# Convolution products moved from GpSimd to ScalarE, with the rotary sines, the even layer's decays, an odd layer's transposes, the layer norm's sums and the first loads rearranged

## The reference, cut to what matters

```
u = x * (1 + sc1) + sh1
proj = u @ w_in                                   # q, k, v, glu_in (1024), two gates (1024 each)
q, k = partial_rope(q, cos, sin), partial_rope(k, cos, sin)
attn = moba_attention(q, k, v)                    # 8 heads of 64, causal over 256 keys
h = a * sigmoid(g)                                # glu, 512 channels
h = depthwise_conv(h, dw_w, 31 taps, causal) + dw_b
y_conv = silu(layer_norm(h)) @ w_conv_pw
y = (sigmoid(g_attn) * (attn @ w_attn_br) + sigmoid(g_conv) * y_conv) @ w_out
x = layer_norm(ALPHA * x + (1 + gt1) * y)         # called ln{l}a below
u = x * (1 + sc2) + sh2
x = layer_norm(ALPHA * x + (1 + gt2) * (relu(u @ w_up)**2 @ w_down))   # ln{l}b
```

## Time and profile before

| | us |
|---|---|
| median of 3 runs | 1769.52 |
| lowest and highest | 1769.32, 1771.22 |
| the profiled execution's own time | 1772.76 |
| its span (first to last instruction) | 1770.9 |
| PE busy | 1732.9 |
| DVE busy | 1378.2 |
| ACT busy | 917.0 |
| POOL busy | 289.3 |

### The profile page before, as it was taken

The page is one execution under the profiler, slowest core; times in us unless marked ns, Lnnn a source line. Parts: engine busy times, 40 slices in busy tenths (PEclk is TensorE's granted clock), DMA queues, the critical chain, the costliest instruction groups (busy, mean ns, idle before and its releaser), DMA issues.

```text
span 1770.9 us, 26710 instructions
## 1 busy us (share of the span) xinstructions
PE 1732.9 (98%) x11234; PEld 1555.7 (88%) x11234; DVE 1378.2 (78%) x1851; ACT 917.0 (52%) x1137; POOL 289.3 (16%) x219
## 2 busy tenths in 40 slices
PE   8999999999999999999999999999999999999998
PEld 7888998888888888879888898898888998998887
DVE  7998754798788988787988779888755599778754
ACT  6554454655355554466554444756543537556432
POOL 1000000220210001050000139600000089100000
PEclk9999999999999999999999999999999999999999
DMA  8666542467666667524676644344455444345552
GB/s 283 242 254 263 211 144 100 171 259 263 233 235 255 261 255 267 214 87 169 259 262 234 250 156 154 120 168 152 182 189 190 144 167 143 142 142 190 188 183 84
DMA packets 53815, 348.15 MB, mean 197 GB/s; under 512 B 6833, under 2 KB 10434, under 8 KB 13762
## 3 DMA queue, kind: packets, MB, share of 16 engines
q1 hardware_dynamic: 53698, 346.46, 53.7%
HBM read 345.39 MB, written 1.05 MB: 196 GB/s over the span
## 4 chain that ended last, share of the span: by engine, by line
PE 86%; DVE 8%; ACT 2%; DMA 1%; POOL 1%; issue 0%; SPq 0%; ACTq 0%; DVEq 0%; POOLq 0%
PE bank L952 40%; PE bank L951 21%; PE bank L904 7%; PE bank L906 6%; PE bank L905 6%; DVE wl L2002 3%; DVE bank L2506 2%; DMA raw<-in_chunks 1%; ACT wh L1524 1%; DVE arena L2553 1%; DVE arena L2525 1%; PE bank L933 1%; PE bank L1467 1%; DVE arena L2524 0%; PE bank L1292 0%
## 5 line engine op out<-in xcount | busy, mean ns | idle before, releaser
L2002 DVE TENSOR_TENSOR wl<-raw,wh 128x2048 fp32r<-128x2048 f32 (+1 forms) x277 | 641.3, 2316 | 226.0 <-ACT wh L1524 224.9
L952 PE MATMUL bank<-xx,wh 128*128 128x512 f32 x1920 | 671.0, 394 | 0.0
L1524 ACT ACTIVATE wh<-raw 128x2048 fp32r<-128x2048 f32 (+1 forms) x277 | 522.3, 1886 | 249.3 <-DMA raw<-in_chunks 249.2
L951 PE MATMUL bank<-xx,wl 128*128 128x256 f32 x1920 | 539.6, 281 | 4.5 <-DVE wl L2038 3.1
L952 PEld LDWEIGHTS bank<-xx,wh 128*128 128x128 f32 x1920 | 359.8, 187 | 81.9
L952 PE MATMUL bank<-hx,wh 128*128 128x512 f32 x1216 | 429.8, 395 | 0.0
L951 PEld LDWEIGHTS bank<-xx,wl 128*128 128x128 f32 x1920 | 362.4, 189 | 7.8 <-issue 4.9
L951 PE MATMUL bank<-hx,wl 128*128 128x256 f32 x1216 | 345.7, 284 | 2.8 <-DVE wl L2002 2.8
L904 PE MATMUL bank<-xx,wh 128*128 128x256 f32 x1008 | 291.2, 289 | 2.9 <-DVE xx L2447 1.5
L905 PE MATMUL bank<-xx,wh 128*128 128x256 f32 x1008 | 285.1, 283 | 0.0
L906 PE MATMUL bank<-xx,wl 128*128 128x256 f32 x1008 | 285.0, 283 | 0.0
(11 more groups left out here) (346 smaller groups left out, 1907.3 us busy)
## 6 DMA issues: line engine op xcount, KB each, us to landing
raw<-in_chunks SPq DMA_DIRECT2D x262, 1024.0 KB, 4.8
arena<-in_ada SPq DMA_DIRECT2D x48, 1024.0 KB, 7.0
raw<-in_chunks SPq DMA_DIRECT2D x16, 768.0 KB, 4.2
arena<-in_bias_rows SPq DMA_DIRECT2D x1, 2048.0 KB, 13.8
x<-in_x SPq DMA_DIRECT2D x4, 256.0 KB, 5.4
raw<-in_chunks SPq DMA_DIRECT2D x4, 256.0 KB, 5.7
arena<-in_w_uk SPq DMA_DIRECT2D x1, 1024.0 KB, 4.8
arena<-in_w_uv SPq DMA_DIRECT2D x1, 1024.0 KB, 8.9
```

The lines of the kernel that those rows point to most:

```text
L951: pe.matmul(o[:, 0:T], lo_w, halves[:, 0, :], start=start, stop=False, skip_group_check=True)
L952: return pe.matmul(o.rearrange("p (h t) -> p h t", h=2), hi_w, halves, start=False, stop=stop, skip_group_check=True)
L1524: act.activation(wh[:, c % RING, at], raw[:, c % RING, at], ACT.Copy).then_inc(hi_made.sem, 1)
L2002: dve.tensor_tensor(wl[:, c % RING, at], raw[:, c % RING, at], wh[:, c % RING, at].bitcast(F32), ALU.subtract).then_inc(lo_made.sem, 1)
```

## The change

It has seven parts.

1. POOL's multiplications in `mix` go to ACT. After its `hi`, ACT makes in steps 4 to 14 the products of 2, 3, 3, 3, 3, 3, 2, 2, 2, 2 and 1 taps, each as two 128x256 activations with a per-partition scale, into a ring of four slots in `xn`. POOL only adds. Tap j of ACT waits for POOL's addition j - 4.
2. `act_rope` is cut in two: the sine after (g, j) = (1, 0), the cosine's after (2, 0).
3. In `EVEN`, `gk` comes before chunk 2, and `G` and `decay` before chunk 3.
4. In `odd`, both halves of chunk 2 come before the transposes of the head weights.
5. The layer norm works on rows (128x256) throughout: PE sums squares and x with the ones matrix, ACT copies the mean row to SBUF (`late_row`), variance, root and reciprocal are 128x256, and the spreading matmuls are gone. One `keep_clock` of 18 follows the sums.
6. The centring reads `late_row` in SBUF; the one of tiles 4 and 5 moves behind the reciprocal, in `dve_mod` after tile 1 (that of tiles 6 and 7 after tile 3), in the last norm just behind the reciprocal.
7. The start loads `x` and chunk 0 in halves (512 KB per DMA) instead of quarters. ACT and DVE still split by quarters.

```diff
+    product = xn[:, :, :].rearrange("p (i c) t -> p i c t", c=2)
-    EVEN = [0, "small", 1, "z", 2, "gk", 3, "G", "decay", 4, 5, "kt", ...]
+    EVEN = [0, "small", 1, "z", "gk", 2, "G", "decay", 3, 4, 5, "kt", ...]
+    PRODUCTS = {4: 2, 5: 3, 6: 3, 7: 3, 8: 3, 9: 3, 10: 2, 11: 2, 12: 2, 13: 2, 14: 1}
...
-        for q in range(4):
-            sp.dma_start(x[:, 2 * q:2 * q + 2, :], A["x"][:, 2 * q:2 * q + 2, :]).then_inc(x_loaded[q].sem, 16)
-            sp.dma_start(raw[:, 0, quarter(q)], A["chunks"][0, :, quarter(q)]).then_inc(first_loaded[q].sem, 16)
+        for q in range(2):
+            sp.dma_start(x[:, 4 * q:4 * q + 4, :], A["x"][:, 4 * q:4 * q + 4, :]).then_inc(x_loaded[q].sem, 16)
+            sp.dma_start(raw[:, 0, half_chunk(q)], A["chunks"][0, :, half_chunk(q)]).then_inc(first_loaded[q].sem, 16)
... pool_mix
-            with pool.Fori(0, (POOL_TAPS - 1) // 2) as g:
-                for b in range(2):
-                    w = vecT[...].unsqueeze(2).broadcast_to((P, 2, T))
-                    pool.tensor_tensor(ptmp[:, b, :, :], hpad[:, 2:4, ...], w, ALU.mult).then_inc(pool_step.sem, 1)
-                    pool.wait_ge(pool_step.sem, g * 4 + (first + 3 + 2 * b))
-                    pool.tensor_tensor(acc, acc, ptmp[:, b, :, :], ALU.add).then_inc(pool_step.sem, 1)
+            for j in range(1, POOL_TAPS):
+                pool.wait_ge(product_made.sem, product_made.at(s, j))
+                pool.wait_ge(pool_step.sem, n_step[0])
+                pool.tensor_tensor(acc, acc, product[:, (j - 1) % 4, :, :], ALU.add).then_inc(pool_step.sem, 1)
+                n_step[0] += 1
... pe_odd
             half_chunk(2, 0)
+            half_chunk(2, 1)
             head_weights()
-            half_chunk(2, 1)
... pe_ln
+            def total(at, src, k, start, stop):
+                return pe.matmul(at, ones[:, :], src[:, k, :], start=start, stop=stop)
             pe.wait_ge(x_ready.sem, xr(s, 6))
+            total(LATE, x, 6, True, False)
             pe.wait_ge(sq_made.sem, sq_made.at(s, 4))
+            total(SQUARES, xn, 6, True, False)
+            pe.wait_ge(x_ready.sem, xr(s, 7))
+            total(LATE, x, 7, False, True).then_inc(late_sum.sem, 1)
             if s[3] == "a":
                 for k in (4, 5):
+                    total(SQUARES, xn, k, False, False)
             pe.wait_ge(six_folded.sem, six_folded.at(s))
+            total(SQUARES, sixq, 0, False, False)
             pe.wait_ge(sq_made.sem, sq_made.at(s, 5))
+            total(SQUARES, xn, 7, False, True).then_inc(stat_made.sem, 1)
-            keep_clock(6)
-            pe.wait_ge(inv_made.sem, inv_made.at(s))
-            ... RSTD spread, keep_clock(7)
             if s != STAGES[-1][1]:
+                keep_clock(18)
... act_ffn
-                if s == "ffn1" and (g, j) == (0, 1):
-                    act_rope()
+                if s == "ffn1" and (g, j) in ((1, 0), (2, 0)):
+                    act_rope(*((sinT, 1) if g == 1 else (cosT, 3)))
... act_mod
-            if KIND[before] == "ln":
-                act.activation(rstd[:, :], RSTD, ACT.Copy).then_inc(rstd_made.sem, 1)
... act_mix
+            def products(n):
+                for _ in range(PRODUCTS.get(n, 0)):
+                    tap[0] += 1
+                    j = tap[0]
+                    if j == 1:
+                        act.wait_ge(glu_made.sem, glu_made.at(s))
+                    if j > 4:
+                        act.wait_ge(pool_step.sem, pool_conv[s] - (POOL_TAPS - 1) + j - 4)
+                    for i in range(2):
+                        last = act.activation(product[:, (j - 1) % 4, i, :], hpad[:, 2 + i, j:j + T], ACT.Copy,
+                                              scale=vec(2 + l, j * CT + 2 + i))
+                    last.then_inc(product_made.sem, 1)
                     act_chunk(s, step, c0 + step, ACT.Sigmoid if step in (2, 3) else ACT.Copy, pm)
+                    products(step)
             def gates(n):
                 act_chunk(s, n, c0 + n, ACT.Sigmoid, pm)
+                products(n)
... act_ln
+            act.wait_ge(late_sum.sem, late_sum.at(s))
+            act.activation(late_row[:, :], LATE, ACT.Copy, scale=1.0 / D).then_inc(late_copied.sem, 1)
+            act.activation(dsq[:, :], LATE, ACT.Square, scale=1.0 / D).then_inc(dsq_made.sem, 1)
             act.wait_ge(var_made.sem, var_made.at(s))
+            act.activation(root[:, :], dsq[:, :], ACT.Sqrt, bias=epsc[:, 1:2]).then_inc(root_made.sem, 1)
... dve_mod
-                if KIND[before] == "ln" and k == 2:
-                    dve_centred(before, 3)
+                if KIND[before] == "ln" and k in (1, 3):
+                    dve_centred(before, 2 + k // 2)
... dve_centred, dve_ln
+            dve.tensor_tensor(xs, xs, late_row[:, :].unsqueeze(1).broadcast_to((P, 2, T)), ALU.subtract).then_inc(cen_made.sem, 1)
+            dve.wait_ge(late_copied.sem, late_copied.at(s))
             dve_centred(s, 0)
+            dve.scalar_tensor_tensor(out=dsq[:, :], in0=SQUARES, scalar=1.0 / D, in1=dsq[:, :], op0=ALU.mult,
                                      op1=ALU.subtract).then_inc(var_made.sem, 1)
             dve_centred(s, 1)
             dve.wait_ge(root_made.sem, root_made.at(s))
+            dve.reciprocal(rstd[:, :], root[:, :]).then_inc(rstd_made.sem, 1)
-            dve_centred(s, 2)
             if s == STAGES[-1][1]:
+                dve_centred(s, 2)
                 dve_centred(s, 3)
                 dve_ln_gain(s)
```

89 lines of the change are left out of this document (27 added, 62 removed).

## The result

| | before | after |
|---|---|---|
| median of the 4 + 4 runs of the comparison, us | 1770.22 | 1752.14 |
| lowest and highest | 1769.32, 1771.22 | 1750.62, 1753.05 |
| ratio, 95% interval | | 0.9897 (0.988 to 0.9914) |
| profiled execution, its span | 1772.76, 1770.9 | 1752.26, 1750.5 |
| mean granted clock | 0.993 | 0.996 |

The change is faster by 18.1 us in the first comparison. It was repeated twice: ratio 0.9915 (0.9899 to 0.9932) and 0.9902 (0.9887 to 0.9917). Over all runs the medians lie 16.0 us apart. Forecast were 11.5: the direction was right, and 4.5 to 6.6 us are missing.

A forecast was written before the change was run, and what follows sets the result against it. The prediction took PE's matmul stream plus PE's pauses and slow running as the bound. Its terms summed to -11.5 us, from the profiled 1772.76 to 1761.3, or 1758.0 as a median 3.2 lower; range 1752 to 1766.5.

The forecast's parts named there:

- Part 3, even: In even, PE's 2.47 us pause before `G` goes: -2.4 us, bounds -1.5 and -2.5.
- Part 2, the sines: In ffn1, PE's 2.81 us pause and 3.1 us of low clock behind it both go: -5.9 us.
- Part 7: At the start, loading in halves instead of quarters gives -0.5 us, bounds -3 and +3.
- the good case: At the start, the last half of chunk 0 lands near 11.3, which gains 0.9 us.
- Rival C: The start loses: late first matmul near 9.4, low clock, late last half; +4.5 instead of -0.5, 1763 us, chance 0.10.
- Part 4: In odd, PE's 0.93 us pause for DVE's last `small` product goes: -0.9 us, bounds 0 and -0.9.
- Part 1: In both mix, products moved to ACT give -2.7 and -3.3, together -6.0 us, bounds -8.4 and 0.
- the two signs of being wrong: In mix: PE waits for ACT's evacuations, or POOL's additions average over 2.5 us.
- Rivals A and B: In mix: A, the ring holds ACT, 1772 us, chance 0.08; B, the convolution gives nothing, 1764 us, chance 0.18.
- Parts 5 and 6: The norms get slower by 0.7, 1.2, 0.7 and 1.6: +4.2 us, bounds +3.0 and +6.0.
- Rival D: More comes back: all pauses of mix and 2 us at the start, 1754 us, chance 0.12.

The follow-up runs named there:

- e10: The changed kernel with the old order of even put back; 1758.40 us, 10 runs, ratio 0.9936 to the kernel before.
- e15: e10 with nine 128x128 matmuls into a free bank before `G` in even; 1755.57 us.
- e13: e9 with eight 128x128 matmuls into a free bank behind the norm's spread in even; 1752.22 us.
- e18: e13 with one convolution tap's product moved from step 10 to step 4; 1750.29 us, 6 runs, ratio 0.9906 to the kernel before.
- e3: The kernel before with only the two sines set apart; ratio 0.9979 to the kernel before.
- e11: The changed kernel with both sines together as before; 1757.31 us, 7 runs, ratio 0.9929 to the kernel before.
- e17: The kernel before without POOL's 26 products and additions per mix, left out of the result; run once for the profile, 1760.33 us.
- e6: The changed kernel with all norms as they were before; 1752.73 us, 6 runs, ratio interval 0.9897 to 0.9941.
- e9: The changed kernel with only the last of the four norms as in the kernel before; 1752.80 us, 6 runs.
- e8: The kernel before with one 128x128 matmul added after every fourth step of each up projection; 1774.19 us in its one execution.
- e1: The kernel before with only the first loads in halves; ratio 0.9983 to the kernel before.
- e2: The kernel before with only the new order of even; ratio 0.9971 to the kernel before.
- e12: The kernel before, unaltered, run once more for its profile; profiled execution 1769.24 us.

## Why the prediction fell short

The table has the terms as means over all 20 profiles: those with a part against those without, by the steps of the shift. For the norms it is the sum of four fixed steps, given below, less the low clock behind them. The last column is the share of a term that is low clock:

```
part                 forecast   first pair    mean with less mean without      of it low clock
                                of profiles   (number of profiles)
7 start                -0.5       -1.3        -1.5 (12, 8)                       +0.2
3 even                 -2.4       -5.6        -5.5 (11, 9)                       -3.2
2 sines                -5.9       -5.9        -2.8 (12, 8)                       -1.1
4 odd                  -0.9       -1.7        -1.5 (12, 8)                        0
1 convolution          -6.0       -6.1        -5.8 (11, 6)                        0
5, 6 norms             +4.2         --        +1.8 (11, 9)                       -1.7
sum                   -11.5                  -15.3
```

The sum, -15.3, stands beside 16.0 between the medians of all runs. The forecast's own additions are right; its terms were not.

- **Part 3, even, is the step that failed.** The forecast said "The pause goes: -2.4 us" and took the pause for all. The pause went: e10 has 2.49 us of it again. But PE lost 4.9 us to low clock in even with the old order (3.4 to 6.8 in nine profiles) and 1.7 with the new (0 to 5.1 in eleven). The forecast charged low clock only behind ffn1's pause and put it at nothing here; the windows over even, which it did not count, had clock 0.95. So of the 5.5 us, 2.3 are the pause, as forecast, and 3.2 are low clock. Why the new order keeps the clock up is open: filling the pause before `G` changed nothing (e15), and the later pause near 290 (285 with the new order) is there in both orders. That later pause is where the largest share lies: low clock comes there in nine of nine profiles with the old order, in six of nine with the new, and in neither of e13 and e18, which fill it. Filling it in the old order was not tried.
- **Part 2, the sines, was right in the pair of profiles and too large in general.** -2.81 and -3.1 came from rows of one execution. Of eight profiles with the old sines four had low clock there (3.4, 1.7, 1.7, 1.7) and three had no pause to speak of, since the pause depends on when a chunk's weights land. The mean is -2.8 by the profiles; the times of e3 and e11 give 2.5 to 5.1, depending on how they are compared.
- **Part 7** was mis-sized: "I take -0.5", its own best case -0.9; it is -1.5. The last half landed before 10.7, where I had 11.3 as the good case. The page on the setup cost that the forecast named was on the right side (the Trainium skill, "SBUF — State Buffer", The DMA setup-cost knee): by that rule fewer and larger loads of the same bytes end sooner, and the trace agrees in direction. Its 8 us, an estimate without any overlap, did not show: the last load landed some 2.7 us sooner (13.43 against 10.7 or earlier). Rival C came true in its first half: the first matmul on chunk 0 comes at 9.3 to 10.0 in the twelve profiles with the new start, and in two of them low clock follows it. The last half was not late, though, so the part still gains.
- **Part 4** was too small: -1.5 for -0.9. PE's bracket was 0.93. What the other 0.6 is was not traced.
- **Part 1** was right in the sum and wrong inside. Against the mean of the profiles without it, contention was worth 9.7 us over both mix (e17), not 8.4. ScalarE's products take back 1.9 (forecast 0.8 + 0.4 per mix, 2.4), and 2.0 stay as contention of additions that still average 1.98 us. DVE's `lo` regained half of its loss, as forecast (2.90 to 2.58 us, of 2.29 without POOL), but PE regained 7.7 of the 9.7. Of the two signs of being wrong, the additions stayed below 2.5 us. PE does wait for ACT's evacuations, but little more than before: 0.43 us at 1097.82, where the forecast had 0.4, and 1.04 in place of 0.71 at 1120.53. Rivals A and B did not come about.
- **Parts 5 and 6**: across each norm, between profiles of equal pace, 0.4, 0.9, 0.6 and 1.6 against 0.7, 1.2, 0.7 and 1.6, hence +3.5. What was missed is on the other side: with the old norms six of nine profiles have low clock at an entry behind a norm (1.7 us on average), with the new form none of eleven. e6's profile has such a stretch (1.7 us at 1180), which fits that it gained nothing measurable. It does not explain e9, whose three inner norms are new: its profile lost 5.1 us to low clock in even, and its six runs can't resolve the 1.6 us expected.
- **Rival D** (1754, "more comes back") gave nearly the right time for the wrong reason: neither did all pauses of `mix` go, nor did the start give 2 us. The measured median, 1752.14, lies at the lower end of the range.
- **The reference execution.** The shown profile had a slow ffn0 (2.3 us) and 1.7 us of low clock at the start. No other profile with the old start had either (e8 aside, whose added matmuls change the pace). Its own time lay 4.5 us above the median of 83 runs.

## What to carry to other kernels

Add up the granted clock's loss over every stage that an edit touches, not only behind a pause: here it was 3.2 of the 5.5 us that the new order of even gave, and it did not follow the pause that was removed. Before weighing terms of 1 to 3 us, look at more than one profile of the same program: here one pause and its low clock came to 6.2 and 4.2 us in two profiles of the kernel before, and to 0.3 in e11, where the sines stand as there. Compare stretches by the start of the n-th instruction of one kind; where no low clock and no change of pace lay in between, it resolved parts to 0.1 us (-3.1 in mix1 in all eleven profiles with part 1 as in the change), where a dozen timed runs left 3.

## What the hardware showed unexpectedly

- PE's stream of pairs runs at 346.7 or 353.3 ns at the same granted clock, held over a whole stage and flipped by a single added 128x128 matmul in all 14 cases of e8. In the 19 profiles without breaks, 8 of 76 ffn stages were slow and 26 of 38 sq stages; the same program differs between executions (sq0 of the changed kernel fast once, slow twice). The cause was not found; whether one matmul added at the right place turns a slow stage into a fast one was not tried.
- Low clock while PE then waits for another engine costs nothing: in e1, e2, e3 and e12 some 1.7 us of it lies before the transposes of each mix, and the shift at the stage's end is the same within 0.4 us as in the profile without it.
- The changed kernel's times scatter less (1.4 us standard deviation in 13 runs) than those of the kernel before (3.4 in 83). A likely reason, not tested, is that places where low clock or a late chunk came by chance are gone.
